# An encoder layer with 32 routed experts on one core: four stage boundaries rewritten, with parts of the residual as TensorE products behind the router

## The chip, the cores and the metric

The kernel runs as one program on 1 core of one Trainium2 chip. The metric is device time in microseconds (us), of which lower is better. Engines are called as the profile calls them: PE (TensorE matmul), PEld (its weight loads), DVE (VectorE), ACT (ScalarE), POOL (GpSimd), SP (SyncE, which here only starts DMAs). A letter q behind an engine means its sequencer, for instance while it issues a DMA.

## What is computed

One layer on 256 tokens of 1024 channels, in fp32:

```python
x = x + token_mixer(rmsnorm(x, g_mix), ...)      # SSD branch and attention branch, gated, then @ w_out
h = rmsnorm(x, g_ffn)
logits = h @ w_router + b_router                 # 32 experts
top_val, top_idx = lax.top_k(logits, 4); top_w = softmax(top_val)
for e in experts:                                # only tokens that chose e
    hm = h[tokens] @ w_mlp1[e] + b_mlp1[e]       # (1024, 2048)
    gate, up = min(hm[:, :1024], 7), clip(hm[:, 1024:], -7, 7)
    y += top_w * ((gate * sigmoid(1.702 * gate) * (up + 1)) @ w_mlp2[e] + b_mlp2[e])
x = x + y
return rmsnorm(x, g_final)
```

The expert weights are 12 MB each, 384 MB in all (402.7 million bytes).

## The kernel before

Every engine has its own program, written by hand, and the order of work is the order of these lines; engines meet through semaphores (`wait_ge`, `then_inc`). There is no scheduler.

**Mixer.** The 36 projection units (`unit`, 1 MB of weights each, 256 output columns, K in 8 steps of 128) run on PE one after another, out of a ring of 10 slots that SP fills. Before the first unit stands the first norm: `xres` holds x with tokens on partitions; ACT squares it (L773), POOL makes the reciprocal root (L956 and L957), DVE scales x into `hN` (L987), PE transposes it (`to_T`, L412), DVE multiplies by the gain into `hT` (L998). SP starts no weight load before x and the small parameters have landed (L334 to L336). The last four units are the output projection (`U_O`, L432 with `tokens=hT`); they wait for all four `mix_ready`. DVE adds each to `xres` (L1165): this is x1, the residual stream.

**Router stretch.** Behind the last unit the same norm is made again: ACT squares (L883), POOL root, DVE scaling (L1169), 16 transposes (L412), DVE gain (L998), 32-column router products (L587). DVE finds the four largest logits and a 0/1 mask `msk` (L1180 to L1201), PE ranks the tokens of each expert with five fp32 products (L592 to L596) and transposes the weights (L599), DVE builds the placement `slotP` of expert 0 (L1232 to L1234). Meanwhile ACT and DVE split the normed rows into three bf16 parts `hb` (L886, L1176, L888, L1211, L895). PE gathers expert 0's tokens into `x32` with 48 bf16 products (`gather`, L607), writes the bias products wT x b2 into the four sums in PSUM (banks 4 to 7, L694), and begins expert 0.

**Experts.** 32 experts at 64 token slots. Weights come in pairs of ring slots, 2 MB a pair, 6 pairs an expert (4 up, 2 down), 8 pairs in the ring; SP starts a pair when the two units before it in that place are used (`unit_used`). Per expert PE does 8 up units (L625), 8 transposes (L659), the sums of the expert before (`combine`, L620), the gather for the next one (L607) and 4 down units (L625) with 2 slot transposes (L614) between them. 16 records of L625 are one pair.

**End.** The last `combine` follows the last expert; DVE adds the four sums to `xres` (L1294), all engines pass a branch for overfull experts (not taken here), ACT squares (L942), POOL root, DVE scales by `g_final` (L1332), SP writes the output in two halves.

## Time and profile before

| | |
|---|---|
| median of 3 runs | 1284.03 us (1283.96 to 1285.02) |
| profiled execution, own time | 1284.34 us |
| its span | 1282.5 us, so 1.84 us lie around it |
| PE busy | 1167.1 us (91%) |
| DVE, ACT, POOL busy | 364.4, 193.2, 19.9 us |
| HBM read | 443.62 MB |

Mean busy shares mislead here, since the kernel has two parts with different limits: up to about 350 us PE works without a break while DMA has pauses, and behind that DMA moves some 428 GB/s without a break while PE waits a little for each pair. A granted clock (PEclk) of 1.00 is 2.4 GHz, 0.50 is 1.2 GHz. A row of the timeline gives the start, the duration, the engine, the line, what is written and read, the count (x), and in brackets the idle time before it with its releaser. fp32 products have two records each, transposes one.

### The profile page before, as it was taken

Reading aid. Unit: us, or ns where it says so; the run is one execution under the profiler, and the core shown is the slowest. Engines: PE = TensorE matmul, PEld = TensorE weight load, DVE = VectorE, ACT = ScalarE, POOL = GpSimd, SP = SyncE. Lnnn points to the kernel's source line nnn. Section 1 sums busy time; section 2 is a strip of 40 time slices with the busy share of each in tenths; the row PEclk is TensorE's granted clock in tenths of the full one; section 3 lists DMA queues with packets and bytes.
Section 4 is the critical chain, followed back from the end, with each engine's and each line's share of the span. In section 5 each row is a group of like instructions: output and inputs, shape, how many; then the busy total and the mean of one; then the engine's idle time right before and its main releaser. Section 6 shows DMA issues by size and latency. Waiting matters only on the chain.

```text
span 1282.5 us, 17137 instructions
## 1 busy us (share of the span) xinstructions
PE 1167.1 (91%) x6736; PEld 584.3 (46%) x6736; DVE 364.4 (28%) x1018; ACT 193.2 (15%) x362; POOL 19.9 (2%) x32
## 2 busy tenths in 40 slices
PE   5999999998799999999998999889889989998885
PEld 5888888887533333333333333333333333333331
DVE  2505788120511222111221211111112212111112
ACT  1212344000210111002111110100021111101001
POOL 0001111000000000000000000000000000000000
PEclk9999999999599999999999999999999999999998
DMA  9943332446189999999999999999999999999993
GB/s 277 303 142 114 130 99 99 169 148 265 63 358 430 426 427 429 428 429 428 429 428 428 429 427 429 429 428 429 428 429 429 428 428 428 429 428 428 427 427 151
DMA packets 68813, 445.16 MB, mean 347 GB/s; under 512 B 6151, under 2 KB 43371, under 8 KB 44171
## 3 DMA queue, kind: packets, MB, share of 16 engines
q1 hardware_dynamic: 65376, 441.47, 83.7%
q10 hardware_dynamic: 3403, 3.22, 0.9%
q8 instruction: 24, 0.39, 0.1%
q14 instruction: 10, 0.08, 0.0%
HBM read 443.62 MB, written 1.05 MB: 347 GB/s over the span
## 4 chain that ended last, share of the span: by engine, by line
PE 54%; DMA 40%; DVE 2%; ACT 2%; issue 1%; ACTq 1%; DVEq 0%; POOL 0%; SPq 0%; POOLq 0%
DMA ring<-in_w_mlp_dram 40%; PE bank L625 24%; PE bank L429 14%; PE bank L432 5%; PE bank L620 3%; PE bank L607 2%; PE bank L659 1%; PE bank L558 1%; PE bank L548 1%; ACT arena L909 1%; PE bank L694 1%; PE bank L520 1%; PE bank L412 1%; PE bank L614 0%; PE bank L587 0%
## 5 line engine op out<-in xcount | busy, mean ns | idle before, releaser
L625 PE MATMUL bank<-ring,arena 128*64 128x512 f32 x3072 | 689.3, 597 | 58.0 <-DMA ring<-in_w_mlp_dram 56.5
L625 PEld LDWEIGHTS bank<-ring,arena 128*64 128x64 f32 x3072 | 209.8, 137 | 489.4 <-issue 369.8
L1252 DVE TENSOR_TENSOR arena<-bank,b1T 128x256 f32<-128x256 f32 x128 | 53.7, 420 | 605.2 <-PE bank L659 602.8
L429 PE MATMUL bank<-hT,ring 128*128 128x256 f32 x576 | 126.1, 379 | 0.8 <-DVE hT L998 0.8
L429 PEld LDWEIGHTS bank<-hT,ring 128*128 128x128 f32 x576 | 109.3, 190 | 16.0 <-DVE hT L998 1.2
L432 PE MATMUL bank<-ring,hT 128*128 128x256 f32 x320 | 72.1, 386 | 2.2 <-DVE hT L1159 2.2
L906 ACT ACTIVATE arena<-bank 128x512 f32<-128x512 f32 x32 | 19.1, 597 | 348.5 <-PE bank L625 348.4
L432 PEld LDWEIGHTS bank<-ring,hT 128*128 128x128 f32 x320 | 61.5, 194 | 11.1 <-DVE hT L1159 2.6
L620 PE MATMUL bank<-arena 64*128 64x512 f32 x264 | 65.6, 615 | 0.8 <-ACT arena L919 0.8
L607 PEld LDWEIGHTS bank<-slotP,hb 128*128 128x128 bf16 x1536 | 47.7, 99 | 27.1 <-issue 23.5
L607 PE MATMUL bank<-slotP,hb 128*128 128x64 bf16 x1536 | 51.5, 195 | 3.1 <-DVE arena L1234 3.1
L659 PE MATMUL bank<-cst,arena 128*128 128x128 f32 x256 | 40.6, 286 | 14.3 <-ACT arena L906 9.6
L659 PEld LDWEIGHTS bank<-cst,arena 128*128 128x128 f32 x256 | 26.8, 140 | 47.1 <-ACT arena L906 36.1
L1232 DVE TENSOR_SCALAR slotP<-cst,rankm 128x64 bf16<-128x64 f32 x64 | 15.8, 247 | 96.9 <-ACT arena L917 96.9
L913 ACT ACTIVATE arena<-arena 128x256 f32<-128x256 f32 x64 | 26.7, 417 | 80.5 <-DVE arena L1254 80.4
L919 ACT ACTIVATE arena<-bank 128x512 f32<-128x512 f32 x32 | 19.1, 597 | 105.5 <-PE bank L625 105.5
L917 ACT ACTIVATE arena<-bank 128x256 f32<-128x256 f32 x32 | 12.3, 384 | 140.8 <-PE bank L614 140.8
L620 PEld LDWEIGHTS bank<-arena 64*128 64x128 f32 x264 | 22.7, 186 | 22.6 <-issue 20.9
L906 ACT ACT_TABLE_LOAD x8 | 10.3, 1283 | 129.2 <-PE bank L625 129.2
L429 PE MATMUL bank<-arena,ring 128*128 128x256 f32 x128 | 28.3, 380 | 0.5 <-ACT arena L867 0.5
L1257 DVE SCALAR_TENSOR_TENSOR arena<-arena 128x256 f32<-128x256 f32 x64 | 27.2, 426 | 2.4 <-DVE arena L1255 0.2
L429 PE MATMUL bank<-over,ring 128*128 128x256 f32 x128 | 27.8, 379 | 0.0
(206 smaller groups left out, 635.7 us busy)
## 6 DMA issues: line engine op xcount, KB each, us to landing
ring<-in_w_mlp_dram SPq DMA_DIRECT2D x192, 2048.0 KB, 32.6
ring<-in_w_in_dram SPq DMA_DIRECT2D x24, 1024.0 KB, 10.7
ring<-in_w_br_attn_dram SPq DMA_DIRECT2D x4, 1024.0 KB, 4.9
ring<-in_w_br_ssm_dram SPq DMA_DIRECT2D x4, 1024.0 KB, 4.9
ring<-in_w_out_dram SPq DMA_DIRECT2D x4, 1024.0 KB, 4.9
xres<-in_x_dram ACTq DMA_DIRECT2D x1, 1024.0 KB, 4.8
out_dram<-hN SPq DMA_DIRECT2D x2, 512.0 KB, 2.7
cst<-shape_constants_dram ACTq DMA_DIRECT2D x1, 736.0 KB, 6.4
```

Source lines behind the costliest of these rows:

```text
L429: last = nc.tensor.matmul(o, w[:, k, a * P:(a + 1) * P], rhs[:, k, :], start=(k == 0), stop=(k == KD - 1))
L432: last = nc.tensor.matmul(o, tokens[:, k, a * P:(a + 1) * P], w[:, k, :], start=(k == 0), stop=(k == KD - 1))
L607: last = nc.tensor.matmul(bank[b][:, k * CAP:(k + 1) * CAP], hb[part][:, t, k * P:(k + 1) * P], slotP[:, par, t, :], start=(t == 0 and par ...
L620: return nc.tensor.matmul(bank[b0 + q][:, :], slotWT[rows, (q // 2) * P:(q // 2 + 1) * P], ysb[rows, :], start=start, stop=stop, skip_grou ...
L625: return nc.tensor.matmul(bank[b][side * CAP:(side + 1) * CAP, :], tokens, w, start=start, stop=stop, skip_group_check=True)
L659: last = nc.tensor.transpose(bank[b][:, j * P:(j + 1) * P], hs[:, b * 512 + j * P:b * 512 + (j + 1) * P], ident)
L906: nc.scalar.activation(hs[:, 0:512].rearrange("q (i p) -> q i p", i=4), bank[0][:, :].rearrange("q (p i) -> q i p", i=4), ACT.Copy).then_i ...
L913: nc.scalar.activation(sg.rearrange("p (i a s) -> p i a s", i=4, a=2)[:, :, h, :], ga.rearrange("p (i a s) -> p i a s", i=4, a=2)[:, :, h, ...
L919: nc.scalar.activation(ysb, bank[2][:, :], ACT.Copy).then_inc(ys_ready, 1)
L1232: V.tensor_scalar(slotP[:, c % 2, t, :], iota, rk, None, ALU.is_equal)
L1252: step(V.tensor_tensor(o, side(bank[b][:, :]), bias_h.to_broadcast([P, 4, CAP]), ALU.add))
L1257: step(V.scalar_tensor_tensor(u_, u_, 1.0, g_, ALU.add, ALU.mult))
```

## The change

Four boundaries are rewritten; the mixer's middle and the body of an expert stay as they are.

1. **Start.** SP starts x in two halves and the weights behind them, without a wait. The constants come in two parts (identity and ones first), the other small loads later. PE transposes raw x (L432 in the new file) while ACT squares it; DVE makes a diagonal of the root, one PE product spreads it, and DVE applies root and gain together in 8 pieces, each of which releases two products of the first unit (`first_unit`). The 16 transposes of b_mlp1 move behind the fourth unit.
2. **Output projection and router.** The first output unit takes its K steps as `mix_ready` comes. Raw x1 is transposed by quarters between the units (`x1_transposes`), ACT squares it by quarters, and the router products run on it without the norm, which is applied to the logits. The mask comes from `match_replace`; the ranks are bf16 products with a bf16 mask; expert 0 is gathered in fp32 straight from `xres` (`first_gather`), so the three bf16 parts are needed only for expert 1. The bias products move into expert 0, in the place where later experts have `combine`.
3. **Residual in the sums.** Where DVE added the sums to x1 at the end, x1 itself is put into the sums by identity products in fp32: rows of tokens 0 to 127 in four 256-column products, three between router and ranks and one between ranks and first gather (`rows_in_sums`); tokens 128 to 255 in two 512-column products in expert 29 (`add_rows`).
4. **End.** The last up pair and the last down pair of expert 31 are loaded as two halves with a semaphore each. The final norm reads the sums from PSUM by quarters: ACT squares, POOL roots per token half, DVE and ACT scale a quarter each, SP and ACT write four quarters.

```diff
-            sp.wait_ge(x_in, 16)
-            sp.wait_ge(row_in, 16 * 6)
-            sp.wait_ge(b1_in, 16)
+            for t in range(TT):
+                sp.dma_start(xres[:, t, :], x[0, t * P:(t + 1) * P, :]).then_inc(x_in[t], 16)
...
+                r = g - (BODY - 1) * EXP_PAIRS
+                if r in SPLIT_PAIRS:
+                    p = pair_at(g)
+                    sp.dma_start(ring[:, 2 * p, :], half_src(NE - 1, r, 0)).then_inc(pair_full[p], 16)
+                    sp.dma_start(ring[:, 2 * p + 1, :], half_src(NE - 1, r, 1)).then_inc(last_half[SPLIT_PAIRS.index(r)], 16)
+                else:
+                    load_moe(NE // BODY - 1, g)
...
+            pe.wait_ge(first_in, 16)
+            for t in range(TT):
+                pe.wait_ge(x_in[t], 16)
+                for k in range(KD):
+                    nc.tensor.transpose(bank[2 + k // 2][:, (k % 2) * 256 + t * P:(k % 2) * 256 + (t + 1) * P],
+                                        xres[:, t, k * P:(k + 1) * P], ident)
...
+            pe.wait_ge(xdiag_ready, 1)
+            nc.tensor.matmul(bank[7][:, 0:SEQ], ones, sqb, start=True, stop=True).then_inc(xrB_psum, 1)
...
+            def first_out_unit():
+
+                n = U_O
+                mix_full(pe, n)
+                pe.wait_ge(unit_taken, n - 1)
+                w = k_view(mix_slot(n))
+                for u in range(4):
+                    pe.wait_ge(mix_ready, u + 1)
+                    for a in range(2):
+                        for k in (2 * u, 2 * u + 1):
+                            last = nc.tensor.matmul(bank[n % 2][:, a * 256:(a + 1) * 256], hT[:, k, a * P:(a + 1) * P], w[:, k, :],
+                                                    start=(k == 0 and a == 0), stop=(k == KD - 1), skip_group_check=True)
+                last.then_inc(unit_done, 1)
+
...
+            def x1_transposes(u):
+
+                pe.wait_ge(unit_taken, U_O + u + 1)
+                for kk in range(2):
+                    o = bank[0][:, 0:256] if (u, kk) == (3, 1) else bank[2 + u][:, kk * 256:(kk + 1) * 256]
+                    for t in range(TT):
+                        last = nc.tensor.transpose(o[:, t * P:(t + 1) * P],
+                                                   xres[:, t, u * UW + kk:(u + 1) * UW:2], ident)
+                last.then_inc(h2T_psum, 1)
...
+            first_out_unit()
+            unit(U_O + 1, tokens=hT)
+            x1_transposes(0)
+            unit(U_O + 2, tokens=hT)
+            x1_transposes(1)
+            pe.wait_ge(late_in, 16 * 2)
+            router(0)
+            unit(U_O + 3, tokens=hT)
+            x1_transposes(2)
+            router(1)
+            x1_transposes(3)
+            router(2)
+            router(3).then_inc(lg_psum, 1)
...
+            def rows_in_sums(q, h):
+
+                o = slice(h * 256, (h + 1) * 256)
+                nc.tensor.matmul(bank[SUMS + q][:, o], ident, fin(xres, q)[:, o], start=(h == 0), stop=False, skip_group_check=True)
...
+            rows_in_sums(0, 0)
+            rows_in_sums(0, 1)
+            rows_in_sums(1, 0)
+            pe.wait_ge(msk_ready, 1)
+            nc.tensor.matmul(bank[7][:, 0:NE], m_leb[:, :], msk[:, 0, :], start=True, stop=True)
+            nc.tensor.matmul(bank[7][:, NE:2 * NE], onesb[:, :], msk[:, 0, :], start=True, stop=False)
+            nc.tensor.matmul(bank[7][:, NE:2 * NE], m_leb[:, :], msk[:, 1, :], start=False, stop=True)
+            nc.tensor.matmul(bank[7][:, 2 * NE:3 * NE], onesb[:, :], msk[:, 0, :], start=True, stop=False)
+            nc.tensor.matmul(bank[7][:, 2 * NE:3 * NE], onesb[:, :], msk[:, 1, :], start=False, stop=True).then_inc(rank_psum, 1)
+            rows_in_sums(1, 1)
+
+            def first_gather():
+
+                pe.wait_ge(p_ready, 1)
                 for k in range(KD):
...
+                    for t in range(TT):
+                        last = nc.tensor.matmul(bank[3 - k // 4][:, (k % 4) * CAP:(k % 4 + 1) * CAP], xres[:, t, (k // 2) * UW + k % 2:(k // 2 + 1) * UW:2],
+                                                slot0[:, t, :], start=(t == 0), stop=(t == TT - 1))
...
+            def add_rows(q):
+
+                nc.tensor.matmul(bank[SUMS + q][:, :], ident, fin(xres, q), start=False, stop=False, skip_group_check=True)
...
+                    if rows_too and q % 2 == 1 and q // 2 >= 2:
+                        add_rows(q // 2)
                 for b in range(2):
                     pe.wait_ge(hs_ready, 2 * e + (b + 1))
                     transposes(b).then_inc(t_psum, 1)
-                pe.wait_ge(ys_ready, e + 1)
-                for q in range(4):
-                    combine(q)
+                if first:
+                    bias_products()
+                    pe.wait_ge(hb_ready, 3)
+                else:
+                    pe.wait_ge(ys_ready, e)
+                    for q in range(4):
+                        combine(q)
                 if not final:
                     pe.wait_ge(p_ready, e + 2)
                     gather((c + 1) % 2, 3).then_inc(x_psum, 1)
...
-            act.wait_ge(unit_taken, N_MIX)
-            for t in range(TT):
-                nc.scalar.activation(hN[:, t, :], xres[:, t, :], ACT.Square, accum_out=stat[:, 20 + t:21 + t]).then_inc(x1sq_ready, 1)
-
-            act.wait_ge(h2_ready, 2)
-            nc.scalar.activation(hb1[:, :, :], hN[:, :, :], ACT.Copy).then_inc(hb_ready, 1)
+            for u in range(4):
+                act.wait_ge(unit_taken, U_O + u + 1)
+                for t in range(TT):
+                    nc.scalar.activation(hs[:, (2 * u + t) * UW:(2 * u + t + 1) * UW], xres[:, t, u * UW:(u + 1) * UW], ACT.Square,
+                                         accum_out=ssq[:, t, u:u + 1]).then_inc(x1sq_ready, 1)
+            act.wait_ge(h2T_psum, 4)
+            nc.scalar.activation(x1T[:, KD - 1, :], bank[0][:, 0:256], ACT.Copy,
+                                 scale=prmT[:, R_GFFN + KD - 1:R_GFFN + KD]).then_inc(x1T_last, 1)
+
+            act.wait_ge(x1r_ready, 1)
+            for t in range(TT):
+                last = nc.scalar.activation(in_row_order(hb1[:, t, :]), by_row_pairs(xres[:, t, :]), ACT.Copy, scale=stat[:, 20 + t:21 + t])
+            last.then_inc(hb_ready, 1)
...
-            act.wait_ge(sum_done, 1)
-            for t in range(TT):
-                nc.scalar.activation(hN[:, t, :], xres[:, t, :], ACT.Square, accum_out=stat[:, 30 + t:31 + t]).then_inc(fsq_ready, 1)
...
+            for q in range(4):
+                act.wait_ge(c_psum, q + 1)
+                nc.scalar.activation(fin(squares, q), bank[SUMS + q][:, :], ACT.Square, accum_out=stat[:, 28 + q:29 + q]).then_inc(fsq_ready, 1)
+            for t in range(TT):
+                q = 2 * t + 1
+                act.wait_ge(fr_ready, t + 1)
+                act.wait_ge(xg_ready, t + 1)
+                nc.scalar.activation(fin(hN, q), fin(hN, q), ACT.Copy, scale=stat[:, 36 + t:37 + t]).then_inc(fin_ready[q], 1)
...
+            last.then_inc(xdiag_ready, 1)
+            dve.wait_ge(xrB_psum, 1)
+            link(V.tensor_copy(rB, bank[7][:, 0:SEQ]))
+            dve.wait_ge(prm_taken, 1)
+            for k in range(KD):
+                V.scalar_tensor_tensor(hT[:, k, :], bank[2 + k // 2][:, (k % 2) * 256:(k % 2 + 1) * 256], prmT[:, R_GMIX + k:R_GMIX + k + 1],
+                                       rB, ALU.mult, ALU.mult).then_inc(hT_ready, 1)
...
+            dve.wait_ge(x1sq_ready, 2 * 4)
+            V.tensor_reduce(stat[:, 20:22], ssq[:, :, :], AXX, ALU.add).then_inc(x1sum_ready, 1)
+            x1T_copy(3)
...
+            link(V.memset(top8[:, :, TOPK:8], NO_LOGIT))
+            for t in range(TT):
+                last = V.match_replace(left36[:, t, :], top8[:, t, :], lg36[:, t, :], PICKED)
             link(last)
-            for t in range(TT):
-                last = V.scalar_tensor_tensor(eqm[:, t, :], eqc[:, t, :], stat[:, 28 + t:29 + t], eqm[:, t, :], ALU.is_le, ALU.mult)
-            link(last)
-            V.tensor_tensor(msk, msk, eqm, ALU.add).then_inc(w_ready, 1)
-            dve.wait_ge(w_ready, 1)
+            V.tensor_tensor(msk[:, :, :], left36[:, :, 0:NE], lgt, ALU.not_equal).then_inc(msk_ready, 1)
+
+            dve.wait_ge(msk_ready, 1)
...
-            V.tensor_copy(cnt[:, 0:1], cnt[:, 0:1]).then_inc(sum_done, 1)
-            dve.wait_ge(fr_ready, 1)
-            dve.wait_ge(gfin_in, 16)
-            for t in range(TT):
-                V.scalar_tensor_tensor(hN[:, t, :], xres[:, t, :], stat[:, 30 + t:31 + t], gfin, ALU.mult, ALU.mult).then_inc(fin_ready, 1)
+
+            dve.wait_ge(gfin_ready, 1)
+            for t in range(TT):
+                dve.wait_ge(c_psum, 2 * t + 2)
+                dve.wait_ge(fsq_ready, 2 * t + 2)
+                V.tensor_tensor(fin(hN, 2 * t + 1), bank[SUMS + 2 * t + 1][:, :], gfin[:, 512:1024], ALU.mult).then_inc(xg_ready, 1)
+                dve.wait_ge(fr_ready, t + 1)
+                V.scalar_tensor_tensor(fin(hN, 2 * t), bank[SUMS + 2 * t][:, :], stat[:, 36 + t:37 + t], gfin[:, 0:512],
+                                       ALU.mult, ALU.mult).then_inc(fin_ready[2 * t], 1)
```

The order of PE's instructions at the start, before; `cst` holds identity and ones, `prm`, `arena` and `dske` small parameters, `over` b_mlp1, `hN` the normed rows:

```order
L393 MATMUL bank<-cst,prm 128x96
L395 MATMUL bank<-cst,arena 128x4 x2
L396 MATMUL bank<-cst,dske 128x8
L402 MATMUL bank<-cst,over 128x32 x16
L412 MATMUL bank<-cst,hN 128x128 x16
L429 MATMUL bank<-hT,ring 128x256 x96
```

and now, where `xres` is x as loaded:

```order
L432 MATMUL bank<-cst,xres 128x128 x16
L436 MATMUL bank<-cst,prm 128x96
L438 MATMUL bank<-cst,arena 128x4 x2
L439 MATMUL bank<-cst,dske 128x8
L441 MATMUL bank<-arena,cst 128x256
L450 MATMUL bank<-hT,ring 128x256 x16
L474 MATMUL bank<-hT,ring 128x256 x48
L459 MATMUL bank<-cst,over 128x32 x16
L474 MATMUL bank<-hT,ring 128x256 x32
```

The transposes of x moved to the front, those of b_mlp1 (`over`) behind the fourth unit.

PE from the last branch unit to expert 0, before:

```order
L429 MATMUL bank<-over,ring 128x256 x64
L432 MATMUL bank<-ring,hT 128x256 x64
L412 MATMUL bank<-cst,hN 128x128 x16
L587 MATMUL bank<-wr,hT 128x32 x16
L592 MATMUL bank<-arena,cst 128x32
L593 MATMUL bank<-arena,cst 128x32
L594 MATMUL bank<-arena,cst 128x32
L595 MATMUL bank<-arena,cst 128x32
L596 MATMUL bank<-arena,cst 128x32
L599 MATMUL bank<-cst,wtok 32x128 x2
```

and now (`m_leb` and `onesb` are bf16 copies of the constants, L726 is expert 0's first product):

```order
L646 MATMUL bank<-cst,xres 128x128 x4
L657 MATMUL bank<-wr,hN 128x32 x8
L678 MATMUL bank<-xres,cst 128x256 x3
L685 MATMUL bank<-msk,m_leb 128x32
L686 MATMUL bank<-msk,onesb 128x32
L687 MATMUL bank<-msk,m_leb 128x32
L688 MATMUL bank<-msk,onesb 128x32
L689 MATMUL bank<-msk,onesb 128x32
L678 MATMUL bank<-xres,cst 128x256
L697 MATMUL bank<-arena,xres 128x64 x16
L829 MATMUL bank<-cst,wtok 32x128 x2
L726 MATMUL bank<-ring,arena 64x512 x32
```

Half of the transposes and a quarter of the router products moved between the output units (ahead of these rows), identity products (L678) stand around the ranks, and the gather (L697) and the transposes of the weights are all that is left ahead of expert 0.

The end of ACT's program, behind the branch for overfull experts, before:

```order
L936 REGISTER_ALU
L938 ACTIVATE arena<-bank 128x512
L929 REGISTER_ALU
L929 COMPARE_AND_BRANCH
L928 UNCONDITIONAL_BRANCH
L942 ACTIVATE hN,stat<-xres 128x1024 x2
L97 UNCONDITIONAL_BRANCH
```

and now:

```order
L1080 COMPARE_AND_BRANCH
L1079 UNCONDITIONAL_BRANCH
L1094 ACTIVATE arena,stat<-bank 128x512 x4
L1099 ACTIVATE hN<-hN,stat 128x512
L1101 DMA out_dram<-hN 128x512
L1099 ACTIVATE hN<-hN,stat 128x512
L1101 DMA out_dram<-hN 128x512
L101 UNCONDITIONAL_BRANCH
```

Two squares of whole rows became four squares read from the sums in PSUM, and two scalings and two output DMAs moved to ACT.

## Rows read from the trace of the kernel before

**Rows 1.** Waits of PE: who was waited for, us in total, times, longest.

```profile
PE bank L625 <- DMA ring<-in_w_mlp_dram: 56.5, 49, 1.3
```

**Rows 2.** Windows: us, busy time of PE, PEld, DVE, ACT, POOL, PEclk, DMA share, GB/s.

```profile
350.00:355.00 5.00, 5.00 (x15) 1.43 (x16) 1.58 (x7) 0.00 (x0) 0.00 (x0) 0.65 0.00 0
...
1100.00:1200.00 100.00, 89.94 (x560) 33.11 (x557) 22.00 (x66) 13.35 (x24) 0.00 (x0) 1.00 1.01 428
```

**Rows 3.** The page, DMA issues: count, KB, us from issue to landing.

```profile
xres<-in_x_dram ACTq DMA_DIRECT2D x1, 1024.0 KB, 4.8
```

**Rows 4.** Timeline at the start.

```profile
10.12 30.14 SPq L340 DMA_DIRECT2D ring<-in_w_in_dram  x11
...
10.83 2.09 PE L402 MATMUL bank<-cst,over 32*128 32x32 f32 x16
...
13.16 0.71 POOL L957 TENSOR_TENSOR stat<-stat 128x2 f32<-128x2 f32 x1
...
19.83 20.34 PE L429 MATMUL bank<-hT,ring 128*128 128x256 f32 x93 [0.78 <-DVE hT L998]
```

**Rows 5.** Timeline of PE, output projection to expert 0.

```profile
287.80 29.58 PE L432 MATMUL bank<-ring,hT 128*128 128x256 f32 x128 [2.23 <-DVE hT L1159]
...
322.90 3.53 PE L412 MATMUL bank<-cst,hN 128*128 128x128 f32 x16 [5.52 <-DVE hN L1169]
...
327.21 4.92 PE L587 MATMUL bank<-wr,hT 128*128 128x32 f32 x32 [0.78 <-DVE hT L998]
...
334.96 0.64 PE L592 MATMUL bank<-arena,cst 128*128 128x32 f32 x2 [2.83 <-DVE arena L1201]
...
340.81 2.74 PE L607 MATMUL bank<-slotP,hb 128*128 128x64 bf16 x48 [3.08 <-DVE arena L1234]
...
343.48 7.19 PE L694 MATMUL bank<-arena 32*128 32x512 f32 x8
...
350.60 15.35 PE L625 MATMUL bank<-ring,arena 128*64 128x512 f32 x64
```

**Rows 6.** Windows of 1 us around the router, columns as in rows 2.

```profile
289.00:290.00 1.00, 1.00 (x4) 0.82 (x3) 0.00 (x0) 0.00 (x0) 0.00 (x0) 0.50 0.92 393
...
325.00:326.00 1.00, 1.00 (x7) 1.00 (x6) 0.84 (x2) 0.00 (x0) 0.00 (x0) 0.50 0.00 0
...
328.00:329.00 1.00, 1.00 (x11) 1.00 (x11) 1.00 (x1) 0.00 (x0) 0.00 (x0) 1.00 0.00 0
...
348.00:349.00 1.00, 1.00 (x3) 0.48 (x2) 0.00 (x0) 0.00 (x0) 0.00 (x0) 0.50 0.00 0
```

**Rows 7.** Chain that ended last, experts 0 to 2: start, us, what.

```profile
367.16 1.15 PE bank L659 x8
368.31 1.92 PE bank L620 x8
370.22 1.51 PE bank L607 x48
...
375.68 17.37 PE bank L625 x80
...
401.81 17.37 PE bank L625 x80
```

**Rows 8.** Timeline from the last up pair to the end.

```profile
1251.99 3.65 PE L625 MATMUL bank<-ring,arena 128*64 128x512 f32 x16 [1.24 <-DMA ring<-in_w_mlp_dram]
...
1267.32 1.99 PE L620 MATMUL bank<-arena 64*128 64x512 f32 x8 [0.78 <-ACT arena L919]
...
1269.38 2.48 DVE L1294 TENSOR_TENSOR xres<-xres,bank 128x512 f32<-128x512 f32 x4 [8.35 <-PE bank L620]
...
1273.62 1.06 ACT L942 ACTIVATE hN<-xres 128x1024 f32<-128x1024 f32 x1 [6.35 <-DVE cnt L1328]
...
1276.90 2.48 DVE L1332 SCALAR_TENSOR_TENSOR hN<-xres,stat,arena 128x1024 f32<-128x1024 f32 x2 [3.31 <-POOL stat L957]
...
1279.41 0.34 SPq L383 DMA_DIRECT2D out_dram<-hN  x1
```

417 lines of the change are left out of this document (236 added, 181 removed).

## The prediction

> **What bounds the kernel now.** I read the waits of TensorE first, then the table of windows, then the timeline at four places. In the waits [rows 1] PE waits for expert weights 49 times, 56.5 us in all and at most 1.3 us at a time, and for little else: weights come as fast as DMA can bring them. The windows say from when [rows 2]: from 350 to 355 us DMA moves nothing, because all 8 pairs of the ring are full and none has been used; from 1100 to 1200 it moves 428 GB/s without a pause. 184 of the 192 pairs (2.097 MB) are moved behind that pause, 4.90 us each, some 901 us whatever PE does. One expert is 6 pairs, 29.4 us of DMA, against 26.1 us of PE work where weights are there (the same stretch of five pairs begins at 375.68 and, one expert on, at 401.81 us [rows 7]). So the time is: the start of the stream (when PE has used its first pair), plus a fixed stream, plus what follows the last pairs. Every us that the first 350 us lose is won in full, if nothing starves the stream behind it. Work inside the stream costs nothing up to 3.2 us an expert.
>
> **Start.** Before, SP begins its weight loads at 10.12 us, behind the small parameters; PE makes 16 transposes of b_mlp1 (2.09 us), the root is ready at 13.9, 16 transposes and gains follow, and the first unit starts at 19.83 [rows 4]. x itself needs 4.8 us from its issue [rows 3]. After: x lands near 5.5 in two halves, ACT has squared it near 7.9 (1.06 a half, as the squares of [rows 8]), POOL needs 0.9 with its scaling step (0.71 for the power alone [rows 4]) and the handover 0.3, DVE's diagonal 0.3, the spreading product and its copy 1.3, the first piece of gain 0.5: 11.3. The transposes of x lie before that, beside ACT. Saved 8.5; bounds 5 (small parameters land at 10 as before, and everything hangs on them) and 9.5. The b_mlp1 transposes now stand inside the mixer, where PE has no pause to hide them: +1.8 (1.0 to 2.1, their old price).
>
> **Output projection.** PE waited 2.23 us for the last `mix_ready`; behind that wait the granted clock is 0.50 at 289 us, and the four units took 29.58 us, where the same products in experts and mixer run at full rate; 64 products at 0.43 are 27.65 [rows 5, 6]. With three quarters of the first unit placed into the wait both go: -2.2 and -1.9. Added between the units are 8 transposes (0.14 each, from 8 in 1.15 [rows 7]) and 4 router products (0.21 to 0.31: 11 records a us at full clock [rows 6], 16 products in 4.92 us at mixed clock [rows 5]): +2.1. Net -2.0 (0 to -3).
>
> **Router stretch.** Before, from the end of the last unit (287.80 + 29.58 = 317.38) to the first product of expert 0 (350.60) are 33.2 us [rows 5]. After, in order: 8 transposes and 12 router products 3.7; the mask 1.8, since DVE's chain of 2.83 (PE's idle time before L592) loses its count, scan and two selections and gets a replacement of like size; five one-pass rank products and their handover 0.7 (fp32 at half clock: some 2.1); placement 0.7, where 3.08 us were idle before L607 because ranks, overflow test and six placements stood in a row; the fp32 gather, 16 products that I price as router products, 3.4; weight transposes 0.3; and 0.9 for a dozen handovers. Sum 11.5. The squares, POOL's root and the bf16 parts lie beside this: the root is needed for the logits only, the parts not before the middle of expert 0. The bias products (7.19) leave the stretch. Saved 21.7. Bounds: 10.0 at the least, 16 if the clock is at half from the ranks on and the gather's strided rows load slowly (0.31 a product or more).
>
> The four **residual products** cost nothing in this sum. A 256-column fp32 product is 0.43: three are 1.3 in the mask's 1.8, the fourth fits the placement's 0.7. At half clock they are 2.6 and 0.85 and stick out by about 1 us together. Below zero they could reach too, if they keep the clock up where PE would pause (up to 2 us, the gather's share in rival B). The two 512-column products in expert 29 (0.86 each) lie in its slack of 3.2.
>
> **The clock** decides the spread. The rows [6] show it: 0.50 at 289 us behind a wait of 2.2 us; 0.50 at 325 with nothing but transposes, 1.00 at 328 right behind them; 0.50 at 348, in the middle of 7.19 us of bias products from 32 partitions, without a pause [rows 5]. So it went up behind transposes and did not go up under these bias products. In the new stretch PE pauses less than 1 us in all, where it had pauses of 5.52, 2.83 and 3.08 [rows 5]; I take 1.00 as the likelier. Then the first pair of expert 0 is also at full rate: its four up pairs took 15.35 us [rows 5], four at 17.37/5 = 3.47 [rows 7] take 13.9, so -1.4 (0 to -1.4).
> The Trainium skill (TensorE: Matmul & The Clock Gate, Part 4: PE-mode transpose) speaks against this: it says that a transpose does not count as busy time for the clock. The row at 328 us disagrees. By that rule the first unit and the router stretch would run at half clock, and the time would be rival B's; a sixth of B's chance is its.
>
> **Expert 0.** The stream starts when its first pair is used, but the fifth must be free in time. Before, pair 1 was used at 355.5 (350.60 + 3.5 + 1.4) and pair 5 at 375.3 (0.4 of slot transposes before 375.68): 19.8 us for four transfers of 4.9, so no slack. Now the bias products (3.6 at full clock, half of 7.19) stand in the place of `combine` (1.92 [rows 7]): pair 5 comes 1.6 later and the stream pauses that long, +1.6. The 512 KB of `g_final`, 1.2 us of the stream, fall into that pause. Bounds +0.5 and +5: at half clock the bias products are 7.19 and what follows is slower too. The second wait placed here, for the three bf16 parts, is covered: they are done some 18 us behind the projection, and PE asks at 27.
>
> **End.** Before, the last up pair is awaited until 1251.99 and used for 3.65 us; half of it is now done while the other half lands: -1.8 (-1.0 to -1.8). The last down pair is no gain, as PE comes to it later than the data. From the last product (1267.32 - 0.78 = 1266.54) to the span's end were 16.0 us: eviction, sums, additions of 2.48, a branch, two squares of 1.06, root, DVE 2.48, output 3.1 from its issue at 1279.41 [rows 8]. After: eviction 0.8, ACT's branch to 2.3, four squares of 0.62 behind it to 4.8, root 5.8, last quarter scaled 6.6, issue 7.0, output 3.1: 10.0. Saved 6.0 (5 to 7).
>
> **The sum**, against the profiled execution (1284.34, of it 1.84 around the span): -8.5 + 1.8 - 2.0 - 21.7 - 1.4 + 1.6 - 1.8 - 6.0 = -38.0, so 1246.3. The median stands 0.31 below that execution: 1246.0.
>
> **Rivals.**
> A, the forecast: full clock, small parameters in time. 1246.0, its own range 1243 to 1248.5.
> B, the clock falls once behind the router or in the middle of expert 0. For: in the one place PE does router, rank and gather products and in the other bias products, and at 348 us it did such work at 0.50 [rows 6]. Against: the pauses between them are short now, and both begin at full rate. Price: the gather 2 us, first pair 1.4 and parts of the ranks; or bias, gather and down products of expert 0 another 2 to 4. Middle 4.5: 1250.5.
> C, a single step is dearer: small parameters behind the big loads (+4 at the start), or the gather from rows with a stride of two (+3): 1249.5. For: the small parameters now share the DMA engines with 10 MB of weights. Against: they are issued 1 us earlier and their queue holds less.
> D, slower than before: the stream stops being the bound. If the clock also fell inside every expert, so that its PE time went from 26.1 over 29.4, each us above would count 31 times. It decides from about two half-clock stretches (1.6 us lost each) in every expert; with three, 31.1 against 29.4, the time is 1246 + 31 x 1.7 = 1299. For: PE waits at every pair. Against: it does so now, and the body of an expert is unchanged.
> E, the change doesn't take effect: ring, queue order or `late_in` hold the first expert where it was. The eighth pair is loaded from the projection's end and is needed only by expert 1, so I see nothing; had it only the end's gain, 1276.
>
> **Chances.** A 0.53, B 0.30, C 0.14, D 0.01, E 0.02. The range reaches over B and C with the lower bounds of the terms: 1242.5 to 1252.5. A measurement of this kernel can tell about 0.2% (2.6 us) from no change; faster 0.98, same 0.01, slower 0.01.
>
> **What would show it.** First unit near 11.3; the last unit's end near 308.7 (317.38 - 8.7); first L726 product near 320 with PEclk 1.00; DMA idle for some 1.5 us in expert 0 and at 428 GB/s behind it; span end some 10 us behind the last expert product. Wrong: PEclk 0.50 in windows behind 312 us (B), a first unit at 15 or later (C), a stream slower than 4.90 us a pair (D).

## The result: faster by 30.6 us, 1.4 us outside the range

| | median us | runs from | to | n |
|---|---|---|---|---|
| before | 1284.53 | 1283.96 | 1287.72 | 4 |
| changed | 1253.92 | 1253.39 | 1255.21 | 4 |

The ratio is 0.9758, with a 95% interval of 0.974 to 0.9776. The forecast was 1246.0 us, with a range of 1242.5 to 1252.5. The sign and most of the gain came as written, 30.6 of the 38.0 us forecast; the time is 7.9 us over the forecast. The changed kernel was timed once more, beside later experiments (e10): 1254.06, ratio 0.9761 (0.974 to 0.9782). The profiled execution took 1255.21 us, 1253.4 of it span; it is the slowest of the four, 1.3 us above the median.

What PE waits for, and windows of the stream and of expert 0 (columns as in rows 2), changed kernel:

```profile
PE bank L726 <- DMA ring<-in_w_mlp_dram: 55.7, 49, 1.5
...
PE bank L685 <- DVE msk L1363: 0.5, 1, 0.5
PE bank L697 <- DVE arena L1369: 0.4, 1, 0.4
```

```profile
346.00:348.00 2.00, 2.00 (x13) 0.84 (x12) 0.69 (x1) 0.00 (x0) 0.00 (x0) 0.52 1.07 459
350.00:355.00 5.00, 5.00 (x24) 1.56 (x22) 1.30 (x6) 0.50 (x2) 0.00 (x0) 1.00 0.82 272
700.00:900.00 200.00, 181.53 (x1118) 66.35 (x1116) 44.01 (x133) 23.52 (x44) 0.00 (x0) 1.00 1.01 428
```

Against [rows 1, 2]: the stream is what it was, 428 GB/s, and PE waits for it 49 times. The two waits behind the router, 2.83 and 3.08 us in [rows 5], are 0.5 and 0.4. From 350 to 355 us, where DMA moved nothing before, it now moves 272 GB/s: it pauses for some 1.8 us, since the fifth pair is late. The clock is at 0.52 in expert 0.

The start, the stretch from the projection to expert 0, and the end, in the timeline of the changed kernel (answers [rows 4, 5, 8]):

```profile
11.85 9.61 PE L450 MATMUL bank<-hT,ring 128*128 128x256 f32 x32 [1.13 <-DVE hT L1158]
```

```profile
283.85 7.07 PE L636 MATMUL bank<-ring,hT 128*128 128x256 f32 x32
...
306.31 7.15 PE L477 MATMUL bank<-ring,hT 128*128 128x256 f32 x32
...
316.83 1.54 PE L678 MATMUL bank<-xres,cst 128*128 128x256 f32 x6
318.83 0.19 PE L685 MATMUL bank<-msk,m_leb 128*128 128x32 bf16 x1 [0.46 <-DVE msk L1363]
...
318.97 0.68 PE L678 MATMUL bank<-xres,cst 128*128 128x256 f32 x2
320.08 3.98 PE L697 MATMUL bank<-arena,xres 128*128 128x64 f32 x32 [0.43 <-DVE arena L1369]
...
324.21 13.95 PE L726 MATMUL bank<-ring,arena 128*64 128x512 f32 x64
...
340.44 3.69 PE L782 MATMUL bank<-arena 32*128 32x512 f32 x8
344.07 2.40 PE L708 MATMUL bank<-slotP,hb 128*128 128x64 bf16 x48
```

```profile
1223.87 7.09 PE L726 MATMUL bank<-ring,arena 128*64 128x512 f32 x32 [1.47 <-DMA ring<-in_w_mlp_dram]
...
1242.48 1.99 PE L721 MATMUL bank<-arena 64*128 64x512 f32 x8 [0.78 <-ACT arena L1068]
1243.64 0.60 ACT L1094 ACTIVATE arena<-bank 128x512 f32<-128x512 f32 x1 [1.21 <-PE bank L721]
...
1248.21 0.35 ACTq L1101 DMA_DIRECT2D out_dram<-hN  x1
```

The three identity products (L678, six instructions, since each fp32 product shows as two) stand in the mask's wait, the fourth behind the rank products. From the projection's end (313.46) to expert 0 are 10.8 us, where 33.2 were.

The terms, each measured between the same two events of both traces:

| stretch | forecast | measured |
|---|---|---|
| start to the branches' end, 285.57 to 283.85 | -6.7 | -1.7 |
| branches' end to the projection's end, 31.8 to 29.6 | -2.0 | -2.2 |
| projection's end to expert 0, 33.2 to 10.8 | -21.7 | -22.5 |
| expert 0 to the landing of the last but one up pair, 896.5 to 899.7 | +0.2 | +3.2 |
| that landing to the last expert product, 19.45 to 17.8 | -1.8 | -1.6 |
| last product to the span's end, 16.0 to 11.7 | -6.0 | -4.3 |
| sum of the span | -38.0 | -29.1 |

(+0.2 is -1.4 for the first four up pairs, at full rate now, and +1.6 for expert 0. 899.7 is 1223.87 - 324.21; 896.5 is 1251.99 - 4.90 - 350.60 of [rows 5, 8], one pair ahead of the last.) Three rows hold the error: the mixer (5.0 us), expert 0 (3.0) and the end (1.7). The projection and the router are 1.0 better than forecast.

### The profile page after: what moved, and what is told of

Its sections match the earlier page's. It is cut to its first block, busy times and chain, and to the rows that moved or that the text cites. A ratio compares the mean times of both kernels' runs of the same rounds, so it can differ in the third digit from the quotient of the medians.

```text
span 1253.4 us, 17033 instructions
## 1 busy us (share of the span) xinstructions
PE 1164.9 (93%) x6721; PEld 584.3 (47%) x6721; DVE 360.6 (29%) x1018; ACT 194.8 (16%) x381; POOL 23.9 (2%) x35
## 4 chain that ended last, share of the span: by engine, by line
PE 55%; DMA 41%; ACT 2%; issue 1%; DVE 1%; ACTq 0%; POOL 0%; SPq 0%; DVEq 0%; POOLq 0%
DMA ring<-in_w_mlp_dram 41%; PE bank L726 25%; PE bank L474 14%; PE bank L477 4%; PE bank L721 3%; PE bank L708 2%; PE bank L773 1%; PE bank L450 1%; PE bank L606 1%; PE bank L596 1%; PE bank L568 1%; PE bank L636 1%; ACT arena L1059 1%; PE bank L715 0%; PE bank L697 0%
## 5 line engine op out<-in xcount | busy, mean ns | idle before, releaser
L726 PE MATMUL bank<-ring,arena 128*64 128x512 f32 x3072 | 688.4, 597 | 57.2 <-DMA ring<-in_w_mlp_dram 55.7
L726 PEld LDWEIGHTS bank<-ring,arena 128*64 128x64 f32 x3072 | 209.6, 137 | 486.7 <-issue 367.4
L474 PE MATMUL bank<-hT,ring 128*128 128x256 f32 x544 | 120.8, 382 | 0.0
L474 PEld LDWEIGHTS bank<-hT,ring 128*128 128x128 f32 x544 | 104.2, 192 | 14.4
L477 PE MATMUL bank<-ring,hT 128*128 128x256 f32 x288 | 63.8, 380 | 0.0
L477 PEld LDWEIGHTS bank<-ring,hT 128*128 128x128 f32 x288 | 54.2, 190 | 7.1
L1443 DVE TENSOR_TENSOR arena<-arena 128x256 f32<-128x256 f32 x64 | 27.2, 425 | 2.2
## 6 DMA issues: line engine op xcount, KB each, us to landing
cst<-shape_constants_dram ACTq DMA_DIRECT2D x1, 608.0 KB, 12.8
```

Of the source, the lines that this page charges most:

```text
L474: last = nc.tensor.matmul(o, w[:, k, a * P:(a + 1) * P], rhs[:, k, :], start=(k == 0), stop=(k == KD - 1))
L477: last = nc.tensor.matmul(o, tokens[:, k, a * P:(a + 1) * P], w[:, k, :], start=(k == 0), stop=(k == KD - 1))
L726: return nc.tensor.matmul(bank[b][side * CAP:(side + 1) * CAP, :], tokens, w, start=start, stop=stop, skip_group_check=True)
L1443: V.tensor_tensor(u_, u_, s_, ALU.mult).then_inc(actT_ready, 1)
```

## The experiments

All edits are to the changed kernel unless the text says otherwise. "Stream time" below is always the time from the first L726 product of expert 0 to the landing of the last but one up pair; in the changed kernel 899.7. The experiments ran in four sets of runs, each beside the kernel before, whose median was 1284.6, 1285.7, 1285.0 and 1285.7 us there; so kernels of different sets are better compared by their ratios than by their medians.

### Without the identity products behind the router (e1)

```diff
-            rows_in_sums(0, 0)
-            rows_in_sums(0, 1)
-            rows_in_sums(1, 0)
...
-            rows_in_sums(1, 1)
...
-                    if rows_too and q % 2 == 1 and q // 2 >= 2:
+                    if rows_too and q % 2 == 1:
                         add_rows(q // 2)
```

> The changed kernel without the four identity products around the ranks; all four sums get x1 in expert 29 (four 512-column products there). Theory 1 (they fill time that PE would wait anyway and do nothing else): first product of expert 0 within 0.2 us of 10.9 us behind the output projection, span within 1 us of 1253.4. Theory 2 (they also keep the clock up): a window with PEclk 0.50 appears between the router products and expert 0, the stretch grows by 1.5 to 4 us, and the span by as much. The additional 1.7 us in expert 29 cost nothing in both.

Measured: 1257.44 (1256.35 to 1259.29), ratio 0.9794 (0.9778 to 0.9811), 3.5 us slower than the changed kernel. The timeline of PE:

```profile
314.38 0.18 PE L682 MATMUL bank<-msk,m_leb 128*128 128x32 bf16 x1 [1.92 <-DVE msk L1359]
...
315.63 7.09 PE L693 MATMUL bank<-arena,xres 128*128 128x64 f32 x32 [0.96 <-DVE arena L1365]
```

Without them PE idles 1.92 and 0.96 us, and the gather behind takes 7.09 us in place of 3.98, at a granted clock of 0.50; the four up pairs of expert 0 then take 15.75 us in place of 13.95. The ranks come no earlier for it: 35.1 us behind the projection's start (314.38 - 279.31), against 35.0 (318.83 - 283.85). So these products cost nothing, and in the changed kernel's profile the gather is at full rate.

### More of them (e2)

```diff
-            rows_in_sums(0, 0)
+            for _ in range(4):
+                rows_in_sums(0, 0)
```

> The changed kernel with the first of the identity products made four times, so that the wait for the mask holds 6 products of 0.43 us (2.6 us) instead of 3. PE waited 0.46 us there with 3 products. Theory 1 (the cover is what PE waits, 0.46 us): the ranks start 0.8 us later and the span grows by 0.8 us. Rival (the stretch is hidden behind something else, for instance the loads of the ring): no growth.

Measured: 1253.09 (1250.36 to 1255.38), ratio 0.975 (0.9731 to 0.9769). The same as the changed kernel within the intervals, with runs 5 us apart. In the profile the router stretch is at 1.00, and the ranks start 35.7 us behind the projection's start (319.95 - 284.29), 0.7 later than in the changed kernel, near the 0.8 of theory 1. The clock fell somewhere else, behind the 16 transposes of b_mlp1 (they end at 44.6 us):

```profile
42.00:44.00 2.00, 2.00 (x16) 1.67 (x14) 0.73 (x2) 1.11 (x2) 0.00 (x0) 1.00 1.10 348
44.00:46.00 2.00, 2.00 (x10) 1.75 (x10) 1.89 (x6) 0.60 (x1) 0.00 (x0) 0.73 1.10 349
46.00:48.00 2.00, 2.00 (x6) 1.55 (x6) 1.63 (x4) 0.00 (x0) 0.00 (x0) 0.50 1.10 347
```

In the changed kernel's own profile it had fallen behind the dt products instead:

```profile
62.00:64.00 2.00, 2.00 (x6) 1.64 (x6) 1.62 (x5) 0.63 (x1) 0.00 (x0) 0.50 0.48 168
```

### The bias products out of expert 0 (e3)

```diff
                 if first:
-                    bias_products()
+                    pe.wait_ge(wT_ready, 1)
+                    pe.wait_ge(route_ready, 1)
                     pe.wait_ge(hb_ready, 3)
...
                     if rows_too and q % 2 == 1 and q // 2 >= 2:
                         add_rows(q // 2)
+                    if rows_too and q == 3:
+                        bias_products()
```

(b_mlp2 then lies in hN, and the second expert's `combine` starts the two sums that the bias products had started.)

> The changed kernel with the four bias products taken out of expert 0 and made in expert 29, where PE has time; b_mlp2 is loaded into hN behind the router. Theory (the products of 32 rows cost 1.8 us more than the sums in their place and let the clock fall, so the fifth pair is free 3.3 us late and the stream pauses): the third of a window at 0.50 near 345 us goes, the fifth pair is free some 5 us earlier (3.7 for the products, 1.6 for the clock), the span falls by 3.0 to 3.5 us, since the stream needs 19.6 us for four pairs and can't use more. Rival (the stream lost its time to something else, for instance the load of g_final or a slow restart): the span falls by less than 1 us.

Measured: 1250.4 (1247.32, 1247.73, 1253.07, 1253.18), ratio 0.9728 (0.9704 to 0.9751). Faster by 3.5 in the median, with intervals that still overlap. The profiled run is one of the dearer ones: it has no pause of DMA and the clock at 1.00 from 326 us on, but the gather at 0.50 (5.75 us), the four up pairs at 15.12 us for 13.95 in a stream time of 898.3, and the first unit at 8.83 us.

### g_final early (e4)

```diff
             act.wait_ge(wT_ready, 1)
-            act.dma_start(gfin, g_final.partition_broadcast(P)).then_inc(gfin_in, 16)
...
+            act.dma_start(gfin, g_final.partition_broadcast(P)).then_inc(gfin_in, 16)
             act.wait_ge(ssq_psum, 1)
```

(POOL scales it there too, ahead of the root of x1.)

> The changed kernel with the 512 KB of g_final loaded and scaled before the output projection instead of inside the stream. Theory (while the stream pauses in expert 0 anyway, 1.2 us of transfer cost nothing): the span stays within 0.3 us of 1253.4. Rival (every byte in the stream counts): the span falls by 1.2 us. POOL's 2.8 us of scaling no longer slow one DVE step from 0.29 to 1.12 us, worth nothing on the path in both.

Measured: 1253.71 (1253.22 to 1256.53), ratio 0.9767 (0.9751 to 0.9783): nothing. In its profile the mixer is undisturbed, the first unit 7.14 us, the projection begins at 279.22 (forecast 278.9) and expert 0 at 319.58. All of that is lost again in expert 0:

```profile
334.74 1.14 PE L773 MATMUL bank<-cst,arena 128*128 128x128 f32 x8 [1.20 <-ACT arena L1056]
335.81 6.21 PE L782 MATMUL bank<-arena 32*128 32x512 f32 x8
341.95 2.74 PE L708 MATMUL bank<-slotP,hb 128*128 128x64 bf16 x48
```

```profile
344.00:346.00 2.00, 2.00 (x18) 1.07 (x17) 0.69 (x1) 0.00 (x0) 0.00 (x0) 0.50 0.36 147
346.00:348.00 2.00, 2.00 (x8) 0.52 (x6) 0.00 (x0) 0.00 (x0) 0.00 (x0) 0.73 0.00 0
348.00:350.00 2.00, 2.00 (x12) 0.68 (x10) 0.00 (x0) 0.11 (x1) 0.00 (x0) 1.00 0.00 0
```

The bias products take 6.21 us at half clock, the fifth pair is free at 349.4, 29.8 after the start of expert 0, and DMA is idle for some 6 us around it (7 GB/s from 345 to 350 us, 318 from 350 to 355). Stream time 902.8. With such a pause g_final is hidden wherever it stands. This is the forecast's rival B at its second place, with its full price.

### A filler ahead of the first unit (e5)

```diff
             nc.tensor.matmul(bank[7][:, 0:SEQ], ones, sqb, start=True, stop=True).then_inc(xrB_psum, 1)
+            nc.tensor.matmul(bank[1][:, 0:256], ident, xres[:, 0, 0:256], start=True, stop=True)
```

> The changed kernel with one more product, identity with 256 columns of x, written to a bank that is overwritten later, behind the product that spreads the root (0.4 us, where PE idles 1.1 us for the first piece of hT). Theory: in the profile of the changed kernel the first unit took 9.6 us where two of the four experiments so far show 7.15 with the same code, so its clock is a matter of the instant; a filler of 0.4 us closes less than half of the pause. Expected -0.5 us (0 to -2.5), 1253.4, and a first unit that still takes 7 to 10 us. Rival: the pause ahead of the unit alone makes it cold; then the unit takes 7.1 in every run and the median is 2.4 lower, 1251.5.

Measured: 1252.04 (1249.24 to 1254.09), ratio 0.9734 (0.9714 to 0.9754). Its interval reaches into that of the changed kernel: inconclusive. The first unit took 7.14 us in this profile and in those of e13 and e15, which have the same filler, but 8.2 to 8.8 in four others that have it (e14, e16, e17, e18). The filler doesn't settle it.

### The output in two halves from SP (e6)

```diff
-            for q in (0, 2):
-                sp.wait_ge(fin_ready[q], 1)
-                sp.dma_start(out[0, (q // 2) * P:(q // 2 + 1) * P, (q % 2) * 512:(q % 2 + 1) * 512], fin(hN, q)).then_inc(out_done, 16)
+            for t in range(TT):
+                sp.wait_ge(fin_ready[2 * t], 1)
+                sp.wait_ge(fin_ready[2 * t + 1], 1)
+                sp.dma_start(out[0, t * P:(t + 1) * P, :], hN[:, t, :]).then_inc(out_done, 16)
...
-                act.dma_start(out[0, t * P:(t + 1) * P, 512:1024], fin(hN, q)).then_inc(out_done, 16)
```

> The output is written by SP alone, in two halves of 512 KB as in the kernel before, not in four quarters from SP and ACT. The span of the changed kernel ends 5.2 us behind the last issue of its output (ACT's, at 1248.21), where in the kernel before it ended 3.1 behind it. Theory: ACT's queue is slower to finish, or the four quarters get into each other's way; with SP's two halves 3.1 come back: the last half is issued at 1248.4 and ends at 1251.6, -1.8 us. Rival: what is left behind the last issue is fixed and grows with the size; the time then stays within 0.5 us, or is 0.5 worse since the halves start later.

Measured: 1255.61 (1251.57 to 1258.18), ratio 0.9768 (0.9744 to 0.9792). In the trace the end is 10.9 us behind the last product, where the profiles of the four-quarter form have 10.5 (e14) to 11.8 (e4). So it lies within their spread, and the two halves gain nothing that can be told. Each half needed 3.9 to 4.0 us from issue to landing, where the same halves needed 2.7 before.

### The last pairs unsplit (e7)

```diff
-SPLIT_PAIRS = (KD // 2 - 1, EXP_PAIRS - 1)
+SPLIT_PAIRS = ()
```

> The last up pair and the last down pair come as one transfer each again, as in the kernel before. Theory: half of the last up pair's products no longer lies beside the landing of its other half: +1.5 to +1.8 us (products of that pair end at 1230.8 in the changed kernel, wait behind it 3.65 us of products), 1255.6. The last down pair adds nothing, because PE comes to it later than the data. Rival: the split transfers are themselves slower, with half the bytes each: 0.

Measured: 1256.9 (1255.08 to 1260.1), ratio 0.9782 (0.9759 to 0.9805), 3.0 over the changed kernel by the medians, with overlapping intervals. The size is better read from the trace, from the landing of the last but one pair (at 1224.05) to the end of the up products:

```profile
1224.05 3.65 PE L726 MATMUL bank<-ring,arena 128*64 128x512 f32 x16 [1.24 <-DMA ring<-in_w_mlp_dram]
1228.95 3.65 PE L726 MATMUL bank<-ring,arena 128*64 128x512 f32 x16 [1.24 <-DMA ring<-in_w_mlp_dram]
```

8.55 us, against 7.09 with the split: 1.5 us, as forecast within 0.3.

### Bias late and more identity products (e9)

The edits of e3 and of e2 together.

> Two edits at once: the bias products are taken out of expert 0 and made in expert 29, and the first of the identity products beside the mask is made four times (1.2 us more of TensorE work in the wait for the mask). Alone the first gave 1250.4, with single runs at 1247.3, 1247.7, 1253.1 and 1253.2; the profile of one at 1253.1 shows a granted clock of 0.5 in the gather, at full rate in expert 0. Theory: the low runs are those in which the clock held in the gather too; more products beside the mask hold it there: all runs near 1247.5, median 1247.5. Rival 1: the clock falls there whatever stands beside the mask, now and then: two levels again, median 1250. Rival 2: the additional products cost their own time, +1.2.

Measured: 1249.22 (1248.05 to 1250.06), ratio 0.972 (0.9703 to 0.9737). That lies between the theory (1247.5) and the first rival (1250). No run is above 1250.1, where e3 had two at 1253, though with four and five runs the two kernels' intervals overlap. The profiled one has no granted clock under 0.97 anywhere before 368 us, and a stream time of 896.8. Two of its windows, gather and expert 0:

```profile
318.00:320.00 2.00, 2.00 (x20) 2.00 (x19) 1.69 (x3) 0.00 (x0) 0.00 (x0) 1.00 0.00 0
344.00:346.00 2.00, 2.00 (x12) 0.72 (x10) 0.62 (x4) 0.00 (x0) 0.00 (x0) 1.00 1.01 426
```

### The changed kernel again (e10)

> The changed kernel once more, unedited, beside the runs that follow. Theory: its granted clock falls for 3 to 7 us in one or two of four places (first unit, behind the 16 narrow transposes of b_mlp1 at 44 us, behind the dt products at 60 us, behind the bias products in expert 0), in which of them differs from run to run; single runs lie between 1250 and 1258, median 1254 to 1255, as the kernel before was 1 us slower in the second set of runs than in the first. Rival: the places are fixed by the program; then all runs lie within 1 us of 1254.

Measured: 1254.06 (1252.76 to 1256.91), ratio 0.9761 (0.974 to 0.9782). The single runs lie where they were expected. It is the same program, and the clock fell in other places. Its profile has the dt stage at 1.00, the gather at half, and expert 0 at 1.00 from 326 us on (its four up pairs took 15.05 us):

```profile
318.00:320.00 2.00, 2.00 (x16) 2.00 (x15) 0.35 (x2) 0.00 (x0) 0.00 (x0) 0.74 0.00 0
320.00:322.00 2.00, 2.00 (x11) 2.00 (x11) 1.55 (x3) 0.00 (x0) 0.00 (x0) 0.50 0.00 0
...
344.00:346.00 2.00, 2.00 (x50) 1.45 (x48) 1.86 (x5) 0.42 (x1) 0.35 (x1) 1.00 1.06 446
```

So the places are not fixed by the program. That the program decides at how many places the clock can fall is how I read the table below; it is not shown by itself.

### Products of the same size from 128 partitions in the bias products' place (e12)

```diff
                 if first:
-                    bias_products()
+                    for q in range(4):
+                        nc.tensor.matmul(bank[SUMS + q][:, :], cst[:, C_ZERO:C_ZERO + P], fin(xres, q), start=(q >= 2), stop=False, skip_group_check=True)
```

(and the bias products in expert 29, as in e3)

> The bias products go to expert 29, and in their place in expert 0 stand four products of the same shape and number (512 columns), but from 128 partitions instead of 32: a block of zeros with the rows of x. Theory 1 (few partitions make the clock fall): no granted clock below 1.00 from 340 to 350 us, these products take 3.7 us, and the time lies where the wait of the fifth pair alone puts it, 1 to 2 us over e9, about 1251.5. Theory 2 (it is the wait and the short transposes ahead of them, or chance): 0.50 in the profile near 345 us as in five of seven profiles with the bias products there, 1253 to 1255.

Measured: 1253.41 (1250.33 to 1253.83), ratio 0.9749 (0.9729 to 0.977). The products took 3.60 us, no fall in expert 0:

```profile
344.00:346.00 2.00, 2.00 (x19) 0.81 (x17) 1.03 (x2) 0.00 (x0) 0.45 (x1) 1.00 0.94 401
```

But e6, e7 and e10 have none there either, with the bias products in place. With one profile of this form this doesn't tell the theories apart. What it does show, with e6 and e7, is the price of 3.7 us of work in expert 0 at full clock: stream times 897.8, 898.0 and 898.1, against 896.8 in e9.

### All four edits (e13) and again (e18)

e9 with g_final early (e4) and the filler (e5).

> e9 (bias products in expert 29, first identity product beside the mask four times) with two more edits: g_final is loaded and scaled before the output projection, where DMA is nearly idle, instead of in the stream of the experts, and one filler product ahead of the first unit as in e5. Theory: without the bias products nothing starves the stream in expert 0, so the 512 KB of g_final cost their 1.2 us there, and they come back: 1.2 under e9; the filler takes part of the cold first unit away: another 0.5. In e9's units 1247.5. Rival: g_final is hidden in the stream anyway, and the filler does nothing: as e9, 1249.2.

> e13 once more, unedited, in this set of runs: 1246.8 to 1248.7 as before if the four edits keep the clock up in expert 0 and in the router in every run; up to 1251 in single runs if e13's five runs were luck.

Measured: 1248.05 (1246.83 to 1248.63), ratio 0.9714 (0.9696 to 0.9732), and the second time 1248.1 (1245.93 to 1249.13), ratio 0.9707 (0.9692 to 0.9721). This beats the changed kernel by some 6 us, with intervals that don't touch. Stream times 895.6 and 895.5: 1.2 to 1.3 less than e9, which is what g_final costs in a stream that has no pause.

### Narrow work spread out (e14)

```diff
-                if n == U_XBC + 3:
-                    b1_transposes()
+                if n < U_Z - 1:
+                    b1_transposes(n - U_XBC - 1)
+                if n == U_Z - 2:
+                    pe.wait_ge(wdt_in, 16)
+                    pe.wait_ge(prm_taken, 1)
+                    dt_products(0)
             pe.wait_ge(prm_taken, 2)
-            for t in range(TT):
...
-            last.then_inc(dt_psum, 1)
+            dt_products(1).then_inc(dt_psum, 1)
```

(on e13; `b1_transposes(i)` makes four of the 16, `dt_products(t)` half of the dt products)

> e13 with the narrow work of the mixer spread out: the 16 transposes of b_mlp1 stand in fours behind units 1 to 4, and the dt products in two halves, behind units 4 and 5. Theory: in three of nine profiles the clock fell right behind the dt products and in one right behind the 16 transposes, 3 to 6 us at half clock, 1.7 to 2 us lost each time; with pieces of 0.5 and 1.8 us it does not fall there: 0.7 us less than e13 in the median, and above all no run more than 1.5 us over the median. Rival: half as long is long enough for a fall, or more places mean more falls: as e13 or slower by 1.

Measured: 1249.34 (1247.15 to 1250.6), ratio 0.9723 (0.9703 to 0.9743). Not better than e13, if anything 1.3 worse. Its profile shows no fall from 18 us on, but single runs are 3.5 us apart, and the spread pieces cost time of their own: from the first unit's end (20.30) to the projection's start (281.95) are 261.65 us, where e13 has 260.73. Spreading brought nothing.

### Products from the first us on (e15)

```diff
+            pe.wait_ge(warm, 1)
+            for _ in range(5):
+                nc.tensor.matmul(bank[1][:, 0:256], hT[:, 0, 0:P], hT[:, 0, :], start=True, stop=True)
             pe.wait_ge(first_in, 16)
...
+            V.memset(hT[:, 0, :], 0.0).then_inc(warm, 1)
```

(on e13)

> e13 with five products of 256 columns on a tile of zeros at the very start, while TensorE has nothing to do until x lands at 5 us (DVE clears the tile). Theory: the first unit is cold where TensorE has idled and made transposes ahead of it; with products from 0.7 us on the clock is up when the transposes begin: first unit 7.15 us, transposes of x not slower, and no run above 1248.5; median 0.8 below e13. Rival: five products five us ahead of the unit don't reach it: the unit takes 7.1 or 8.8 as before, median as e13. Other rival: they push the transposes back and the first unit starts 0.5 later.

Measured: 1247.56 (1246.71 to 1249.15), ratio 0.9704 (0.9691 to 0.9717), e13's time within the noise. The 16 transposes of x (L435) went faster, 2.52 us in place of 3.67, but started 0.65 later; the first unit was at full rate:

```profile
1.18 4.63 PE L430 MATMUL bank<-hT 128*128 128x256 f32 x10 [1.18 <-DVE hT L1152]
5.61 2.52 PE L435 MATMUL bank<-cst,xres 128*128 128x128 f32 x16
...
11.40 7.14 PE L454 MATMUL bank<-hT,ring 128*128 128x256 f32 x32 [0.70 <-DVE hT L1166]
```

Five other kernels have this unit at 7.1 without those products, so one profile proves nothing; and the clock fell behind the dt products this time.

### All quarters of the output from SP (e16)

```diff
-            for q in (0, 2):
+            for q in (0, 1, 2, 3):
```

(on e13; ACT's two output transfers dropped)

> e13 with all four quarters of the output issued by SP in the order 0, 1, 2, 3, none by ACT. Theory: 5.2 us behind ACT's issue are ACT's queue being slower or younger; from SP it is 3.1 to 3.7 behind an issue that comes 0.3 later: -1 to -1.5 us, span end 10.2 behind the last expert product. Rival 1: the four descriptors of one queue go one behind the other: 11.7 or more. Rival 2: what is left is the write itself, whoever issues it: 11.3, as e9.

Measured: 1248.0 (1247.37 to 1248.49), ratio 0.9707 (0.9694 to 0.9721). The end is 11.5 us behind the last product: it is not ACT's queue.

### The four edits without the identity products (e17)

```diff
-            for _ in range(4):
-                rows_in_sums(0, 0)
-            rows_in_sums(0, 1)
-            rows_in_sums(1, 0)
...
-            rows_in_sums(1, 1)
```

(on e13; all rows are added in expert 29)

> e13 without any identity product around the ranks; all four quarters of the rows are added in expert 29. Theory: with nothing to do beside the mask and the placement the clock falls in the ranks and the gather, as in e1, and stays low for 6 to 14 us: 3 to 4 us slower than e13, 1251.5, and PEclk 0.50 between 312 and 326 us. Rival: what cost e1 its 3.5 us was expert 0 behind it with the bias products; without those the router loses 1 us at most, against 1.1 us of products that are saved: 1248.

Measured: 1252.38 (1250.71 to 1253.76), ratio 0.9741 (0.9727 to 0.9755): 4.3 us slower than e18 beside it, with intervals apart. A window of the gather, and its timeline:

```profile
318.00:320.00 2.00, 2.00 (x11) 2.00 (x11) 0.00 (x0) 0.00 (x0) 0.00 (x0) 0.50 0.00 0
```

```profile
317.21 7.09 PE L694 MATMUL bank<-arena,xres 128*128 128x64 f32 x32 [0.96 <-DVE arena L1368]
```

3.1 us are lost in the gather, 2.1 in the four up pairs behind it (16.07 us for 64 instructions in place of 13.95), and 0.6 are won because the repeated products no longer stand ahead of the ranks. This is the clearest single result of the study: 2.2 us of products that compute something, with 1.3 of repeated ones, are worth 4.3 us. They don't keep the clock up in every execution: in e3 and e10, which have them without the repeated ones, the gather took 5.75 and 5.82 us.

## Why the prediction was wrong, point by point

Where the clock fell in each profile (windows of 2 us with a granted clock under 0.97, up to 368 us; the first unit by its duration, 7.1 at full rate):

| profile | first unit | 44 us | dt, 58 to 67 | ranks and gather | expert 0 | projection starts |
|---|---|---|---|---|---|---|
| changed | 9.6 | | fell | | fell, 3.7 of bias | 283.85 |
| e10, same | 8.8 | | | fell | | 281.12 |
| e1 | 7.15 | | | fell | fell | 279.31 |
| e2 | 10.0 | fell | | | fell | 284.29 |
| e3 | 8.8 | | | fell | | 281.04 |
| e4 | 7.1 | | | | fell, 6.2 of bias | 279.22 |
| e5 | 7.1 | | | | fell, 6.0 of bias | 279.47 |
| e6 | 8.8 | | fell | | | 284.28 |
| e7 | 9.5 | | fell | | | 285.61 |
| e9 | 7.1 | | | | | 279.28 |
| e12 | 8.8 | | fell | | | 282.80 |
| e13 | 7.1 | | | | | 279.23 |
| e18, same | 8.2 | | | | | 280.73 |
| e14 | 8.8 | | | | | 281.95 |
| e15 | 7.1 | | fell | | | 282.61 |
| e16 | 8.3 | | | | | 280.85 |
| e17 | 8.8 | | | fell | | 280.88 |

**Start: right within 0.6 us; the mixer behind it, 4.4 us off.** Forecast was a first unit at 11.3 (the steps named add up to 11.2); it began at 11.85 here and at 11.3 to 12.1 in the other profiles, and the projection at 279.2 where nothing disturbed the mixer (forecast 278.9). The step that failed is that the mixer's only new cost was "+1.8" for the transposes; the clock was put at nothing there. The first unit is slow in 11 of the 17 profiles with the new start (by 1.0 to 2.8 us), and the dt products or the transposes of b_mlp1 were followed by a fall in 6 (1.7 to 3.3 us each). Here they are 2.5 (9.61 for 7.14) and 1.7. The forecast priced falls only behind the router and in expert 0; it named the first unit in one sentence, without a price of its own.

The slow first units are of two kinds. In five profiles (the changed kernel, e2, e7, e16, e18) the spreading product ahead of the unit already ran at half rate, 1.22 us: the clock had not risen yet. In the other six (e3, e6, e10, e12, e14, e17) that product took 0.70 us, full rate, and the granted clock is at 0.50 from about 12 to 15 us: it had risen and fell again. Of each kind one, the changed kernel and e10:

```profile
9.49 1.22 PE L441 MATMUL bank<-arena,cst 128*128 128x256 f32 x2 [0.18 <-DVE arena L1152]
```

```profile
9.74 0.70 PE L441 MATMUL bank<-arena,cst 128*128 128x256 f32 x2
11.56 8.83 PE L450 MATMUL bank<-hT,ring 128*128 128x256 f32 x32 [1.13 <-DVE hT L1158]
```

The first unit stands behind 16 transposes of x, five small products and a pause of about 1 us; before, the mixer stood behind 16 transposes of hN and 0.78, and it ran at full rate [rows 4]. The Trainium skill (TensorE: Matmul & The Clock Gate, Part 4: PE-mode transpose) says that a transpose does not count as busy time for the clock. These traces disagree, as the row at 328 us did: in e14 and e17 the last of the 16 transposes of x took 272 and 273 ns, the full-rate time (median 273 in e15), where most took 421, and PE had done nothing but transposes before. So the rule did not have to be believed for the first unit; what was missing was a price for it.

**Output projection and router: right.** -2.2 for -2.0, 10.8 us for 11.5, the four up pairs at 13.95 for 13.9. All products there ran at full rate in this profile, which is in part luck: in e10, the same program, the gather did not (5.82 us for 3.98), and the stretch took 12.8 us.

**The identity products: cost right, worth undersized.** They cost nothing, as the sum has it. The bound "below zero" was put at 2 us; e1 and e17 give 3.5 and 4.3.

**Expert 0: +1.6 forecast, +4.6 measured (3.2 + 1.4 for the first four up pairs).** The place is B's second. The term has two errors, and the fifth pair tells them apart. The changed kernel, then e6, where expert 0 is at full clock:

```profile
346.39 4.40 PE L726 MATMUL bank<-ring,arena 128*64 128x512 f32 x16
350.73 0.44 PE L715 MATMUL bank<-cst,arena 128*128 128x128 f32 x2
```

```profile
346.01 3.65 PE L727 MATMUL bank<-ring,arena 128*64 128x512 f32 x16
349.60 0.44 PE L716 MATMUL bank<-cst,arena 128*128 128x128 f32 x2
```

The fifth pair is used up when the slot transposes begin: 26.5 us behind the first product of expert 0 (350.73 - 324.21), and 25.0 in e6 and e7. Less 3.5 for the first pair, 25.0 is 21.5, as forecast (19.8 + 1.6). So the first error is the clock, 1.6 us here: the bias products themselves ran at full rate (3.69 us), and the gather behind them (2.40 us for 1.57) and the first down pair (4.40 for 3.65) did not. In e4 and e5 the bias products ran slow too (6.21 and 6.03 us), and the fifth pair comes at 29.8. The second error is behind the fifth pair. From there to the landing of the last but one up pair are 873.1 us in the changed kernel, e6 and e7, where the kernel before has 871.9 (896.5 - 24.6, its slot transposes beginning at 375.24). No term of the forecast has this 1.2 us, and its cause stays open. It is not g_final, since e4, which loads it early, has 873.0; and it is not much more than single profiles differ (872.2 in e2, 873.6 in e10).

Stream times sort the two loads. They are 895.5 without bias products and without g_final in the stream (e13, e16, e18), 896.8 with g_final (e9), 898.0 with both, at full clock (e6, e7), and 902.8 to 903.1 with most of that stretch at half clock (e1, e4, e5). So both together cost 2.5 us at full clock. Alone, g_final costs its own transfer, 1.2 to 1.3 us, as the stream then has no pause. Beside the bias products the traces bear the forecast out that g_final lies in the pause: four transfers of 4.9 from 3.5 on end at 23.1, with g_final's 1.2 at 24.3, the fifth pair is free at 25.0, and what is left of the pause is 0.6 us (e7: 377 of 428 GB/s from 350 to 355). With a longer pause, g_final early or late makes 902.8 and 903.1 (e4, e5). No run has the bias products in place, g_final early and the clock up.

The clock is the larger part. The prediction gave B 4.5 us at a chance of 0.30, as one fall in some cases. In fact all eight profiles with the bias products in expert 0 show a slow stretch somewhere (the changed kernel, e1, e2, e4 to e7, e10), each of 1 to 5 us, at five possible places, and in three of them (e6, e7, e10) not at the bias products. In the profiled execution the clock makes 6.3 of the 8.9 us: 0.5 in the spreading product, 2.5 in the first unit, 1.7 behind the dt products, 1.6 in expert 0. That is the cause of most of the miss: **a fall was treated as a case that happens or not, where it should have been a cost with a mean.** An estimate of that mean: from the changed kernel (1254.0) to e13 (1248.1) are 5.9 us, and 2.5 of them are the bias products and g_final at full clock, which leaves some 3.4 us a run.

**Last up pair: right** (-1.5 for -1.8, by e7's trace too).

**End: 11.7 for 10.0.** (The forecast's own steps add up to 10.1.) The squares, the roots and the scaling came even half a us earlier than forecast, ACT's last issue at 6.5 behind the last product (7.0 forecast). The step that failed is "output 3.1 from its issue": it took 5.2. What DMA moved in the end, changed kernel, then before:

```profile
1250.00:1251.00 1.00, 0.00 (x0) 0.00 (x0) 0.00 (x0) 0.00 (x0) 0.00 (x0) 0.50 0.43 162
1251.00:1252.00 1.00, 0.00 (x0) 0.00 (x0) 0.00 (x0) 0.00 (x0) 0.00 (x0) 0.50 0.07 27
1252.00:1253.00 1.00, 0.00 (x0) 0.00 (x0) 0.00 (x0) 0.00 (x0) 0.00 (x0) 0.50 0.03 10
```

```profile
1280.00:1281.00 1.00, 0.00 (x0) 0.00 (x0) 0.00 (x0) 0.00 (x0) 0.00 (x0) 0.50 1.00 406
1281.00:1282.00 1.00, 0.00 (x0) 0.00 (x0) 0.00 (x0) 0.00 (x0) 0.00 (x0) 0.50 0.64 258
```

The bulk is out by 1250.5, and a few packets trail for 2.5 us; before there was no such tail. Neither another queue (e16, 11.5) nor whole rows of 512 KB (e6, 10.9) takes it away, and its length varies: the end is 10.5 to 11.8 us behind the last product in the other profiles of the four-quarter form. Its cause stays open.

**The sum, once more.** Forecast for the profiled span 1244.5. The first unit and the dt fall +4.2, the rest up to the projection's start +0.8 (0.5 of it the slow spreading product), expert 0 +3.0, the end +1.7, the split +0.2, less 1.0 for projection and router: 1253.4, as measured. As a check from the other side: e13 keeps the structure, takes bias products and g_final out of the way and lets the clock fall seldom. From 1246.0, with -1.6 for the bias products, +1.7 for the end and +0.7 for the repeated products, 1246.8 is expected, and 1248.05 and 1248.1 were measured. What is left, 1.3 us, is of the size of a slow first unit.

What stays open: what sets the instant at which the clock falls, whether few partitions matter for it (e12), the 1.2 us of the stream behind the fifth pair, and the output's tail.

## What to carry to other kernels

When a change makes a serial stretch short, work that was of little account (narrow transposes, products on 32 partitions, pauses of 1 or 2 us) becomes a place at which the clock may fall for some us; price each such place with an estimated mean in the sum, not as a rival, and read the granted clock of several kernels' profiles, since one profile shows only one throw. Waits of 1 to 2 us ahead of dense work are a good home for useful products: here 2.2 us of them (3.5 with the repeated ones) were worth 3.5 to 4.3. And a transfer hidden in a pause of the stream shows its price once the pause is gone: g_final made no difference while the stream paused (e4 against e5) and 1.2 to 1.3 us when it did not (e9 against e13).

## What the runs showed of the hardware that was not expected

The same program shows the half clock in other places from one execution to the next: behind the dt products and in expert 0 in one profile, in the first unit and the gather in the other. Single runs of one kernel spread over 1.1 (e16) to 6.6 us (e6). That the clock makes this spread is not shown: the changed kernel's first four runs lie within 1.8 us, and the kernel before, run beside the experiments, spreads over 1.2 to 6.5 us too.

In the first 20 us the column of the granted clock can't always be relied on. In the changed kernel it says 1.00 from 12 to 16 us, where products of the first unit took up to 765 ns for 379 (5 records from 12 to 14 us, 11 from 18 to 20); in e10 it says 0.50 from 12 to 15 us, with products of up to 634 ns.

```profile
12.00:14.00 2.00, 2.00 (x5) 1.64 (x6) 2.00 (x7) 0.00 (x0) 0.00 (x0) 1.00 1.27 378
...
18.00:20.00 2.00, 2.00 (x11) 1.74 (x10) 0.00 (x0) 0.00 (x0) 0.00 (x0) 1.00 1.20 308
```

And 256 KB of output can need 4.8 us from issue to landing where 512 KB needed 2.7 before and 3.9 to 4.0 in e6, with DMA all but idle at the end.
